# Norm's second half: where two weight remainders, two half-tile evictions and the up pairs' weight splits stand

## The chip, the cores and the metric

One core of a Trainium2 chip runs the whole program. The metric is the device time of one execution in microseconds (us); smaller is better. Five engines work in parallel, each through its own queue in program order: TensorE (PE: matrix multiplies, with its weight loads as PEld), VectorE (DVE), ScalarE (ACT), GpSimd (POOL) and SyncE (SP, which here only starts transfers). They meet at semaphores: an instruction waits until a counter has reached a value, and all that stands behind it on its queue waits too.

## The reference, cut

Two layers; each is a token mixer (projection `w_in`, three branches, gates, `w_out`), a layernorm, a gated feed-forward part with a causal convolution over three positions, and another layernorm. 512 prompt tokens and 64 sample tokens run through the same weights. What the change touches:

```python
def layernorm(x, g, b):
    mu = jnp.mean(xf, axis=-1, keepdims=True)
    xc = xf - mu
    var = jnp.mean(xc * xc, axis=-1, keepdims=True)
    return (xc * lax.rsqrt(var + LN_EPS) * g + b).astype(x.dtype)

def conv_ffn(h, prefix, w_up, conv_w, conv_b, w_down):
    a = h @ w_up                              # 1024 -> 2 * 2816
    ext = jnp.concatenate([prefix, a], axis=1)
    c = conv_b + conv_w[0] * ext[:, 0:T]
    for k in range(1, CONV_W):                # CONV_W = 3 taps
        c = c + conv_w[k] * ext[:, k:k + T]
    gate, up = jnp.split(c, 2, axis=-1)
    y = (jax.nn.silu(gate) * up) @ w_down
    return y, ext[:, -(CONV_W - 1):]

for l in range(2):
    x = layernorm(ALPHA * x + token_mixer(x), ln1_g[l], ln1_b[l])
    x = layernorm(ALPHA * x + conv_ffn(x), ln2_g[l], ln2_b[l])
```

## The kernel before, in words

**Layout.** Features lie on the 128 partitions, all 576 tokens on the free axis, in two token halves of 288. `X` is the residual stream in eight feature tiles (`X[:, k]`). Every large product is made three times in rounded fp32: a value is split into a rounded part (hi, made by ACT) and the remainder (lo, made by DVE), and PE adds w_hi x_hi, w_hi x_lo and w_lo x_hi. The split activations are `XH` and `XL` (both named m_XS in the trace).

**Weight units.** A 128-column slice of a weight matrix is one unit. SP fetches it into a raw buffer `WS`, ACT rounds it into `WH` (`weight_hi`, L548), DVE makes the remainder `WL` (`weight_lo`, L1434). A unit that uses raw buffer n is fetched once the remainder of the unit before it in that buffer is done. PE starts a tile when its remainder is there (`w_lo`), when the result bank of the tile's parity is free (`mm_free0` or `mm_free1`) and, in the first tile after a norm, row by row as `n_lo` counts up.

**Tiles.** A full tile is 8 rows x 2 token halves x 3 = 48 multiplies, a half tile 24.

**Norm, second half.** A norm runs token half by token half. While the second half is normalised, PE works on six half tiles of the next stage that only need the first token half: `first_halves`, with weight units u0 to u0+5. The next stage then begins with units u1 and u1+1. `first_halves` is called three times with a norm or an input: for the mixer input of layer 0 (no norm: the rows of x are only split), after norm 1 of each layer (next stage: the up projection), and after norm 2 of layer 0 (next stage: the input of layer 1). On DVE it runs `centre` (L1451, eight rows), `variance` (L1456), `inverse_root` (L1461), then `scaled` (L1468) and `normal_lo` (L1479) for each of eight rows, with the remainders of u0+4, u0+5, u1 and u1+1 strung between. On ACT it runs the squares (L574), the root (L579), `normal_hi` (L593; L548 where there is no norm) for the rows, and evicts each half tile: `stash` copies it to `STASH`, `first_half` copies it to `Z`.

**Up projection.** In up pair j, parity 0 is the gate tile and parity 1 the up tile. Pairs 0, 2 and 4 (`UP_FIRST`) had their first token half done in `first_halves`, so only a half tile of 24 multiplies is left of each; pairs 1, 3, 5 and all later ones are full. `up_tile` exists once on ACT (L940) and once on DVE (L1949). For each parity ACT copies the product to `EB` and rounds the weights of the next pair's tile of that parity; DVE then runs tap two (L1963), tap one (L1970) and tap zero (L1976) of the convolution into `CC`. ACT's Silu (L962) needs the gate half's last tap (`c_ready`). DVE multiplies (`HX`, L1984 and L1985), ACT rounds the product (`HH`), DVE takes its remainder (`HL`). The convolution of a parity starts when its `EB` copies are done, and those copies start when PE has ended the tile.

Of the kernel before, what the change touches and what calls it, by code (L numbers as in the profile page):

```python
# [13 lines left out]
D = 1024  # L14
# [92 lines left out]
def build(nc, x_t, x_save, cache_wide, page_table, branch_in, w_uk, w_ukt, w_uv, state_ffn_t, params,  # L107
# [3 lines left out]
    with ctx:  # L111
# [434 lines left out]
        def _(act):  # L546
# [72 lines left out]
            def first_halves(l, n, u0, m0, u1, evict):  # L619
# [24 lines left out]
                normal_hi(n, 1, (2, 3, 4))  # L644
                done(4)
                evict(4)
                normal_hi(n, 1, (5, 6, 7))
                done(5)
                evict(5)

            for l in range(DEPTH):
# [288 lines left out]
                def up_tile(hf, j, width, halved=None, last=False):  # L940
                    n0 = (l * 2 + hf) * FH + j
                    u0 = l * NU + U_FFN[hf] + 2
                    for par in range(2):
# [16 lines left out]
                        if par == 0:  # L960
                            act.wait_ge(S["c_ready"], n0 + 1)
                            nc.scalar.activation(SL[:, 0:CV - 2], CC[:, 0, 0:CV - 2], ACT.Silu)\  # L962
                                .then_inc(S["silu"], 1)
# [5 lines left out]
                for hf in range(2):  # L969
                    first = 2 * len(UP_FIRST) if hf == 0 else 0  # L970
                    for j in range(first):
                        up_tile(hf, j, D, UP_FIRST.index(j) if j in UP_FIRST else None)
# [459 lines left out]
        def _(dve):  # L1432
# [81 lines left out]
            def first_halves(l, n, u0, u1):  # L1514

                if n >= 0:
                    centre(n, 1, range(DT))
                    variance(n, 1)
                weight_lo(l * NU + u0 + 4)
                if n >= 0:  # L1520
                    inverse_root(n, 1)
                scaled(n, 1, 0)
                scaled(n, 1, 1)
                weight_lo(l * NU + u0 + 5)
                normal_lo(n, 1, 0)
                normal_lo(n, 1, 1)
                scaled(n, 1, 2)
                scaled(n, 1, 3)
                weight_lo(l * NU + u1)
                normal_lo(n, 1, 2)  # L1530
                scaled(n, 1, 4)
                normal_lo(n, 1, 3)
                scaled(n, 1, 5)
                normal_lo(n, 1, 4)
                scaled(n, 1, 6)
                normal_lo(n, 1, 5)
                scaled(n, 1, 7)
                normal_lo(n, 1, 6)
                normal_lo(n, 1, 7)
                weight_lo(l * NU + u1 + 1)  # L1540
# [27 lines left out]
            for l in range(DEPTH):  # L1568
# [380 lines left out]
                def up_tile(hf, j, width, halved=False, last=False):  # L1949
                    n0 = (l * 2 + hf) * FH + j  # L1950
                    u0 = l * NU + U_FFN[hf] + 2 * j
                    for par in range(2):
# [15 lines left out]
                        if halved:  # L1968
# [9 lines left out]
                        if par == 0:  # L1978
                            dve.drain().then_inc(S["c_ready"], 1)
                            if not halved:  # L1980
# [8 lines left out]
                    if not halved and not last:  # L1989
# [5 lines left out]
                for hf in range(2):  # L1995
# [4 lines left out]
                    for j in range(first):  # L2000
                        up_tile(hf, j, D, halved=j in UP_FIRST)
# [183 lines left out]
```

## Time and profile before

| | us |
|---|---|
| median of 3 runs | 2121.1 |
| lowest and highest run | 2120.16 and 2124.65 |
| span of the profiled execution | 2123.8 |
| TensorE busy in it | 2047.8 |
| VectorE busy | 1194.9 |
| ScalarE busy | 804.0 |
| GpSimd busy | 401.2 |

The profiled execution is one more execution of the same program, 2.7 us longer than the median. Busy time of a matmul is modelled and overlaps its neighbours, so a pause of PE between two tiles is a little longer, from start to start, than the idle time that a row gives. In the rows of the next but one section, the square bracket at the end of a row is the idle time of that engine just before the row and what ended it.

### The profile page before, as it was taken

To read this page: it belongs to the slowest core of one execution; us is meant where nothing else is said; L and a number is where in the kernel's file an instruction comes from. 1 tells how busy PE (TensorE), PEld (TensorE's weight loads), DVE (VectorE), ACT (ScalarE), POOL (GpSimd) and SP (SyncE) were. 2 spreads that over 40 slices of the span, in tenths; PEclk is the share of its full clock that TensorE was granted. 3 is DMA by queue.
4 is the path that set the end of the run, shared out by engine and by line. 5 is a ranking of instruction groups with operands and counts; after the bars stand their busy time and mean duration, and the time that the engine had idled before them with its cause. 6 is when DMAs were issued, how large, how long until landed. Compare 5 with 4: busy or idle time off the path is not lost.

```text
span 2123.8 us, 43041 instructions
## 1 busy us (share of the span) xinstructions
PE 2047.8 (96%) x17374; PEld 1891.6 (89%) x17374; DVE 1194.9 (56%) x2032; ACT 804.0 (38%) x1508; POOL 401.2 (19%) x407
## 2 busy tenths in 40 slices
PE   7999999999998999999999999999999999999997
PEld 7976667999998999999989766689999889999997
DVE  4764545333578652666758644453335876436665
ACT  4343434222354321334443443342223543223334
POOL 0026661000051000000350366600002600000012
PEclk9999999999999999999999999999999999999999
DMA  7349996222433232225452599942225232222252
GB/s 253 118 149 328 373 353 232 80 79 80 156 108 96 84 105 67 79 79 181 136 206 68 174 364 365 370 161 88 80 79 175 90 100 79 99 71 82 79 195 73
DMA packets 88850, 325.69 MB, mean 153 GB/s; under 512 B 10576, under 2 KB 15568, under 8 KB 88592
## 3 DMA queue, kind: packets, MB, share of 16 engines
q1 hardware_dynamic: 46512, 169.52, 24.4%
q0 software_dynamic: 37440, 144.98, 18.4%
q10 hardware_dynamic: 4768, 9.37, 1.4%
q8 instruction: 92, 1.51, 0.3%
q14 instruction: 38, 0.31, 0.0%
HBM read 315.52 MB, written 7.26 MB: 152 GB/s over the span
## 4 chain that ended last, share of the span: by engine, by line
PE 84%; DVE 8%; ACT 3%; DMA 2%; issue 1%; DVEq 1%; POOL 0%; PEldq 0%; SPq 0%; ACTq 0%; PEld 0%; POOLq 0%
PE PS L1010 65%; PE PS L1292 5%; PE PS L1262 5%; DVE m_WL L1434 3%; PE PS L1283 2%; DMA m_WS<-in_w_units 1%; PE PS L1273 1%; ACT m_WH L548 1%; DVE m_X L1468 1%; PE PS L1315 1%; DVE m_XS L1479 1%; PE PS L1041 1%; PE PS L1331 1%; PE PS L1322 1%; PE PS L1309 1%
## 5 line engine op out<-in xcount | busy, mean ns | idle before, releaser
L1010 PE MATMUL PS<-m_XS,m_WH 128*128 128x288 f32 x5120 | 922.0, 297 | 34.6 <-DVE m_WL L1434 18.0
L1010 PEld LDWEIGHTS PS<-m_XS,m_WH 128*128 128x128 f32 x5120 | 767.9, 189 | 43.7 <-DVE m_WL L1434 20.9
L1010 PE MATMUL PS<-m_XS,m_WL 128*128 128x288 f32 x2560 | 583.5, 297 | 0.0
L1434 DVE TENSOR_TENSOR m_WL<-m_WS,m_WH 128x1024 fp32r<-128x1024 f32 (+2 forms) x284 | 369.2, 1301 | 229.9 <-ACT m_WH L548 221.0
L548 ACT ACTIVATE m_WH<-m_WS 128x1024 fp32r<-128x1024 f32 (+2 forms) x284 | 315.6, 1113 | 374.6 <-PE PS L1010 341.1
L1010 PEld LDWEIGHTS PS<-m_XS,m_WL 128*128 128x128 f32 x2560 | 423.5, 189 | 0.0
L535 POOL DMA_INDIRECT m_RAW<-in_cache_wide,m_IDXS x256 | 242.4, 947 | 380.2 <-PE PS L1010 124.4
L478 POOL TENSOR_TENSOR m_XS<-m_X 128x288 f32<-128x288 f32 x8 | 10.6, 1320 | 1170.5 <-DVE m_X L1488 1169.5
L1010 PE MATMUL PS<-m_HH,m_WH 128*128 128x288 f32 x704 | 205.7, 299 | 5.2 <-DVE m_X L1488 4.9
L1010 PE MATMUL PS<-m_HL,m_WH 128*128 128x288 f32 x704 | 203.5, 296 | 0.0
L1010 PE MATMUL PS<-m_HH,m_WL 128*128 128x288 f32 x704 | 180.3, 297 | 0.0
L1010 PEld LDWEIGHTS PS<-m_HH,m_WH 128*128 128x128 f32 x704 | 133.0, 189 | 6.3 <-DVE m_WL L1434 5.3
L1010 PEld LDWEIGHTS PS<-m_HL,m_WH 128*128 128x128 f32 x704 | 133.2, 189 | 0.2
L1292 PE MATMUL PS<-m_RAW,m_PT 128*64 128x256 f32 x1024 | 124.6, 385 | 7.4 <-ACT m_PT L548 7.1
L1262 PE MATMUL PS<-m_RAW,m_QSF 64*64 64x256 f32 x1024 | 125.3, 382 | 0.9 <-DMA m_RAW<-in_cache_wide,m_IDXS 0.9
L1262 PE MATMUL PS<-m_RAW,m_QSR 64*64 64x256 f32 x1024 | 124.4, 382 | 0.0
L1010 PEld LDWEIGHTS PS<-m_HH,m_WL 128*128 128x128 f32 x704 | 123.2, 189 | 0.0
L1963 DVE TENSOR_SCALAR m_CC<-m_EB,m_PARS 128x592 f32<-128x592 f32 x88 | 51.9, 590 | 123.5 <-ACT m_EB L548 123.4
L1292 PEld LDWEIGHTS PS<-m_RAW,m_PT 128*64 128x64 f32 x1024 | 67.8, 136 | 47.8 <-ACT m_PT L548 14.6
L902 ACT ACTIVATE m_SIG<-PS 128x576 f32<-128x576 f32 x48 | 31.2, 650 | 185.7 <-PE PS L1010 185.7
L1786 DVE TENSOR_SCALAR_CACHE_REDUCE PS<-PS,m_NMX 128x512 f32<-128x512 f32 x64 | 48.5, 759 | 92.0 <-PE PS L1273 92.0
L1262 PEld LDWEIGHTS PS<-m_RAW,m_QSF 64*64 64x64 f32 x1024 | 69.0, 133 | 28.0 <-issue 16.1
(276 smaller groups left out, 2875.4 us busy)
## 6 DMA issues: line engine op xcount, KB each, us to landing
m_WS<-in_w_units SPq DMA_DIRECT2D x232, 512.0 KB
m_WS<-in_w_units SPq DMA_DIRECT2D x48, 704.0 KB
m_RAW<-in_cache_wide,m_IDXS POOLq DMA_INDIRECT x256
m_X<-in_x_t SPq DMA_DIRECT2D x6, 576.0 KB, 7.4
m_WS<-in_w_units SPq DMA_DIRECT2D x4, 576.0 KB
x_save<-m_X POOLq DMA_DIRECT2D x4, 576.0 KB, 4.4
m_X<-x_save SPq DMA_DIRECT2D x4, 576.0 KB, 6.9
out_y<-m_X SPq DMA_DIRECT2D x8, 288.0 KB, 2.2
```

The costliest lines, as they stand in the source:

```text
L535: pool.indirect_dma_start(raw_of(u)[:, q, :], None, cache_wide.rearrange("l n c -> (l n) c"), bass.IndirectOffsetOnAxis(ap=IDXS[:, l, g:g ...
L548: return nc.scalar.activation(out, in_, ACT.Copy)
L902: nc.scalar.activation(h2(SIG[:, g, :]), pair(g % 2), ACT.Sigmoid)\
L1010: mm = pe.matmul(out(half), w(part, k), x(k)[:, half_of(half)], start=(k == 0 and part == 0 and x is xh), stop=(k == last and part == 1))
L1041: mm = pe.matmul(PS[:, bank + h, 0:HT], C["ones"], x[:, h * HT:(h + 1) * HT], start=(k == 0), stop=(k == len(tiles) - 1))
L1262: pe.matmul(PS[64 * c:64 * c + 64, score_bank(u) + h, 0:256], weights, raw_of(u)[rows, c::2, at0:at0 + P], start=(g == 0), stop=False)
L1273: mm = pe.matmul(out[:, :, j, :], QSP[j][rows, rows_of], raw_of(u)[rows, c::2, 2 * KL:ROW], start=False, stop=(j == 1))
L1283: mm = pe.transpose(PS[:, 6, j * P:(j + 1) * P], PRB[:, j * P:(j + 1) * P], ident)
L1292: mm = pe.matmul(PS[64 * c:64 * c + 64, 7, 0:KL], PT[:, a, 64 * c:64 * c + 64], raw_of(u)[:, 2 * (a // 2) + c, j * KL:(j + 1) * KL], start ...
L1434: return dve.tensor_tensor(out, x, hi.bitcast(F32), ALU.subtract)
L1786: dve.tensor_scalar(s0, s0, -SCALE, NMX[:, b, j:j + 1], ALU.mult, ALU.min, accum_out=NMX[:, b, j + 1:j + 2]).then_inc(S["s_max"], 1)
L1963: dve.tensor_scalar(cc, e[:, 2:CV], tap(2), PARS[:, bass.ds(l * NPAR + C_CB + c, 1)], ALU.mult, ALU.add)
```

## The change

**Norm's second half, DVE.** The remainders of u0+4 and u0+5 move ahead of `variance`, that of u1 to right behind it. The rows follow in strict alternation, one `normal_lo` between two `scaled`, and the remainder of u1+1 moves from the end to ahead of the last two `normal_lo`.

**Norm's second half, ACT.** Half tile 4 is evicted after two rounded rows instead of five, half tile 5 after five instead of eight.

**Up pairs.** On DVE, pairs 0 to 5 of the first feed-forward half all take the weight remainders between tap two and tap one (before: pairs 0, 2 and 4 only). On ACT, Silu of these six pairs stands behind the up half's copies and weight rounding instead of behind the gate half's.

```diff
@@ first_halves, ACT
                 weight_hi(l * NU + u1 + 1)
                 normal_hi(n, 1, (0, 1))
-                normal_hi(n, 1, (2, 3, 4))
                 done(4)
                 evict(4)
-                normal_hi(n, 1, (5, 6, 7))
+                normal_hi(n, 1, (2, 3, 4))
                 done(5)
                 evict(5)
+                normal_hi(n, 1, (5, 6, 7))
@@ up_tile, ACT
-                        if par == 0:
+                        if par == (1 if silu_last else 0):
                             act.wait_ge(S["c_ready"], n0 + 1)
...
-                        up_tile(hf, j, D, UP_FIRST.index(j) if j in UP_FIRST else None)
+                        up_tile(hf, j, D, UP_FIRST.index(j) if j in UP_FIRST else None, silu_last=True)
@@ first_halves, DVE
                     centre(n, 1, range(DT))
+                weight_lo(l * NU + u0 + 4)
+                weight_lo(l * NU + u0 + 5)
+                if n >= 0:
                     variance(n, 1)
-                weight_lo(l * NU + u0 + 4)
+                weight_lo(l * NU + u1)
...
@@ up_tile, DVE
-                        up_tile(hf, j, D, halved=j in UP_FIRST)
+                        up_tile(hf, j, D, early=True)
```

On DVE after norm 1 of layer 0, behind the eight rows of `centre`, the queue is the following before; m_WL 152, 153, 154 and 155 are the remainders of u0+4, u0+5, u1 and u1+1.

```order
L1451 SCALAR_TENSOR_TENSOR m_X<-PS,m_X 128x288 x8
L1456 TENSOR_SCALAR m_RN<-PS 128x288
L1434 TENSOR_TENSOR m_WL_152<-m_WS_137,m_WH_144 128x1024
L1461 RECIPROCAL m_RN<-m_RN 128x288
L1468 SCALAR_TENSOR_TENSOR m_X<-m_X,m_PARS,m_RN 128x288 x2
L1434 TENSOR_TENSOR m_WL_153<-m_WS_138,m_WH_145 128x1024
L1479 SCALAR_TENSOR_TENSOR m_XS_50<-m_X,m_PARS,m_XS_50 128x288 x2
L1468 SCALAR_TENSOR_TENSOR m_X<-m_X,m_PARS,m_RN 128x288 x2
L1434 TENSOR_TENSOR m_WL_154<-m_WS_139,m_WH_146 128x1024
```

The same place after:

```order
L1451 SCALAR_TENSOR_TENSOR m_X<-PS,m_X 128x288 x8
L1434 TENSOR_TENSOR m_WL_152<-m_WS_137,m_WH_144 128x1024
L1434 TENSOR_TENSOR m_WL_153<-m_WS_138,m_WH_145 128x1024
L1456 TENSOR_SCALAR m_RN<-PS 128x288
L1434 TENSOR_TENSOR m_WL_154<-m_WS_139,m_WH_146 128x1024
L1461 RECIPROCAL m_RN<-m_RN 128x288
L1468 SCALAR_TENSOR_TENSOR m_X<-m_X,m_PARS,m_RN 128x288 x2
L1479 SCALAR_TENSOR_TENSOR m_XS_50<-m_X,m_PARS,m_XS_50 128x288
L1468 SCALAR_TENSOR_TENSOR m_X<-m_X,m_PARS,m_RN 128x288
```

Two remainders have passed the variance, a third the reciprocal, and none stands between the rows any more until the last two.

On ACT, behind the root of the same norm (m_WH_147 is u1+1 rounded), the queue is before:

```order
L548 ACTIVATE m_WH_147<-m_WS_140 128x1024
L593 ACTIVATE m_XS_50<-m_X,m_PARS 128x288 x5
L548 ACTIVATE m_STASH<-PS 128x288
L593 ACTIVATE m_XS_50<-m_X,m_PARS 128x288 x3
L548 ACTIVATE m_STASH<-PS 128x288
L938 ACT_TABLE_LOAD
```

and after:

```order
L548 ACTIVATE m_WH_147<-m_WS_140 128x1024
L593 ACTIVATE m_XS_50<-m_X,m_PARS 128x288 x2
L548 ACTIVATE m_STASH<-PS 128x288
L593 ACTIVATE m_XS_50<-m_X,m_PARS 128x288 x3
L548 ACTIVATE m_STASH<-PS 128x288
L593 ACTIVATE m_XS_50<-m_X,m_PARS 128x288 x3
L938 ACT_TABLE_LOAD
```

Each of the two evictions has moved ahead of three rounded rows.

On DVE in up pair 1 of layer 0, which is a full pair, the queue is before (m_WL_152 and m_WL_153 are the remainders for pair 2, parities 0 and 1):

```order
L1963 TENSOR_SCALAR m_CC<-m_EB,m_PARS 128x592
L1965 COPY m_TAIL<-m_EB 128x2
L1970 SCALAR_TENSOR_TENSOR m_CC<-m_EB,m_PARS,m_CC 128x592
L1972 COPY m_TAIL<-m_EB 128x16
L1976 SCALAR_TENSOR_TENSOR m_CC<-m_EB,m_PARS,m_CC 128x592
L1434 TENSOR_TENSOR m_WL_152<-m_WS_137,m_WH_144 128x1024
L1963 TENSOR_SCALAR m_CC<-m_EB,m_PARS 128x592
```

and after:

```order
L1964 TENSOR_SCALAR m_CC<-m_EB,m_PARS 128x592
L1966 COPY m_TAIL<-m_EB 128x2
L1434 TENSOR_TENSOR m_WL_152<-m_WS_137,m_WH_144 128x1024
L1971 SCALAR_TENSOR_TENSOR m_CC<-m_EB,m_PARS,m_CC 128x592
L1973 COPY m_TAIL<-m_EB 128x16
L1977 SCALAR_TENSOR_TENSOR m_CC<-m_EB,m_PARS,m_CC 128x592
L1964 TENSOR_SCALAR m_CC<-m_EB,m_PARS 128x592
```

The remainder has moved ahead of tap one; in parity 1 of the pair it moves likewise, from behind `HX` to ahead of tap one.

## Rows read from the trace of the kernel before

**Rows 1.** The page: busy time, share of the span and instructions of each engine.

```profile
PE 2047.8 (96%) x17374; PEld 1891.6 (89%) x17374; DVE 1194.9 (56%) x2032; ACT 804.0 (38%) x1508; POOL 401.2 (19%) x407
```

**Rows 2.** Timeline, PE, layer 0's up stage: start, us, engine, line, operation, [idle before].

```profile
639.76 0.51 PE L1010 MATMUL PS<-m_XS,m_WH 128*128 128x288 f32 x2 [1.67 <-issue]
...
644.42 0.54 PE L1010 MATMUL PS<-m_XS,m_WH 128*128 128x288 f32 x2 [0.47 <-DVE m_WL L1434]
...
661.25 0.54 PE L1010 MATMUL PS<-m_XS,m_WH 128*128 128x288 f32 x2 [0.72 <-DVE m_WL L1434]
...
666.16 0.54 PE L1010 MATMUL PS<-m_XS,m_WH 128*128 128x288 f32 x2 [1.45 <-DVE m_WL L1434]
...
687.91 0.54 PE L1010 MATMUL PS<-m_XS,m_WH 128*128 128x288 f32 x2 [2.06 <-DVE m_WL L1434]
```

**Rows 3.** Timeline, DVE, norm's second half, layer 0.

```profile
628.65 0.46 DVE L1456 TENSOR_SCALAR m_RN<-PS 128x288 f32<-128x288 f32 x1 [6.10 <-PE PS L1063]
...
643.15 1.22 DVE L1434 TENSOR_TENSOR m_WL<-m_WS,m_WH 128x1024 fp32r<-128x1024 f32 x1
```

**Rows 4.** Timeline, ACT, same place.

```profile
625.46 1.06 ACT L548 ACTIVATE m_WH<-m_WS 128x1024 fp32r<-128x1024 f32 x1
...
639.27 0.39 ACT L548 ACTIVATE m_STASH<-PS 128x288 f32<-128x288 f32 x1
```

**Rows 5.** Chain that ended last, in order of time, at layer 1's input.

```profile
1071.23 4.95 DMA m_WS<-in_w_units
...
1082.94 5.89 PE PS L1010 x24
```

**Rows 6.** Timeline, layer 1's input: DVE's variance, ACT's rounding of u1+1, PE.

```profile
1069.53 0.46 DVE L1456 TENSOR_SCALAR m_RN<-PS 128x288 f32<-128x288 f32 x1 [6.37 <-PE PS L1063]
...
1076.20 1.06 ACT L548 ACTIVATE m_WH<-m_WS 128x1024 fp32r<-128x1024 f32 x1 [3.11 <-DMA m_WS<-in_w_units]
...
1082.94 0.82 PE L1010 MATMUL PS<-m_XS,m_WH 128*128 128x288 f32 x2 [3.59 <-issue]
```

**Rows 7.** Windows: us, busy (and count) of PE, PEld, DVE, ACT, POOL; clock, DMA, GB/s.

```profile
689.10:692.40 3.30, 3.30 (x16) 3.30 (x15) 2.89 (x4) 0.22 (x2) 0.00 (x0) 0.50 0.69 197
...
1081.60:1088.40 6.80, 5.46 (x23) 5.49 (x24) 6.41 (x10) 2.73 (x6) 6.46 (x7) 0.50 0.55 178
...
1736.00:1741.00 5.00, 2.93 (x22) 2.76 (x21) 4.79 (x9) 2.43 (x6) 0.00 (x0) 1.00 0.31 96
```

**Rows 8.** Windows of PE alone: us, busy (count), clock; a half tile at either clock.

```profile
661.20:664.50 3.30, 3.25 (x24) 1.00 0.48 159
...
687.90:692.70 4.80, 4.79 (x24) 0.64 0.55 160
```

**Rows 9.** Timeline, DVE, up pair 1 of layer 0, parity 1, then pair 2.

```profile
661.49 0.59 DVE L1963 TENSOR_SCALAR m_CC<-m_EB,m_PARS 128x592 f32<-128x592 f32 x1 [0.29 <-ACT m_EB L548]
...
662.23 0.84 DVE L1970 SCALAR_TENSOR_TENSOR m_CC<-m_EB,m_PARS,m_CC 128x592 f32<-128x592 f32 x1
...
664.15 0.69 DVE L1984 TENSOR_TENSOR m_HX<-m_SL,m_CC 128x512 f32<-128x512 f32 x1
...
664.89 1.22 DVE L1434 TENSOR_TENSOR m_WL<-m_WS,m_WH 128x1024 fp32r<-128x1024 f32 x1
...
667.47 1.23 DVE L1434 TENSOR_TENSOR m_WL<-m_WS,m_WH 128x1024 fp32r<-128x1024 f32 x1
```

**Rows 10.** Timeline, ACT, same place: HH, then copies and rounding for pair 2.

```profile
665.01 0.68 ACT L548 ACTIVATE m_HH<-m_HX 128x576 fp32r<-128x576 f32 x1 [2.68 <-DVE m_HX L1985]
665.60 0.20 ACT L548 ACTIVATE m_EB<-m_SFT 128x16 f32<-128x16 f32 x1
...
666.38 1.06 ACT L548 ACTIVATE m_WH<-m_WS 128x1024 fp32r<-128x1024 f32 x1
```

**Rows 11.** Timeline, layer 0's input: ACT's eviction of half tile 5, DVE's last rows.

```profile
34.85 0.41 ACT L548 ACTIVATE m_Z<-PS 128x288 f32<-128x288 f32 x1 [0.90 <-PE PS L1010]
...
33.00 2.29 DVE L1434 TENSOR_TENSOR m_XS<-m_X,m_XS 128x288 fp32r<-128x288 f32 x6
```

More of the change, by code:

```diff
@@ L938, in _, with up_tile @@
                 nc.scalar.preload_act_table(ACT.Silu)
-                def up_tile(hf, j, width, halved=None, last=False):
+                def up_tile(hf, j, width, halved=None, last=False, silu_last=False):
                     n0 = (l * 2 + hf) * FH + j
@@ L1523, in first_halves @@
                 scaled(n, 1, 1)
-                weight_lo(l * NU + u0 + 5)
                 normal_lo(n, 1, 0)
+                scaled(n, 1, 2)
                 normal_lo(n, 1, 1)
-                scaled(n, 1, 2)
                 scaled(n, 1, 3)
-                weight_lo(l * NU + u1)
                 normal_lo(n, 1, 2)
@@ L1537, in first_halves @@
                 scaled(n, 1, 7)
+                weight_lo(l * NU + u1 + 1)
                 normal_lo(n, 1, 6)
                 normal_lo(n, 1, 7)
-                weight_lo(l * NU + u1 + 1)
             def split_in(half, k):
@@ L1948, in _, with up_tile @@
                     dve.memset(EB[:, par, 0:2], 0.0)
-                def up_tile(hf, j, width, halved=False, last=False):
+                def up_tile(hf, j, width, early=False, last=False):
                     n0 = (l * 2 + hf) * FH + j
@@ L1967, in up_tile @@
                         dve.drain()
-                        if halved:
+                        if early:
                             weight_lo_in_loop(u0 + 2 + par, par, width)
@@ L1979, in up_tile @@
                             dve.drain().then_inc(S["c_ready"], 1)
-                            if not halved:
+                            if not early:
                                 weight_lo_in_loop(u0 + 2, 0, width)
@@ L1988, in up_tile @@
                         .then_inc(S["h_ready"], 1)
-                    if not halved and not last:
+                    if not early and not last:
                         weight_lo_in_loop(u0 + 3, 1, width)
```

## The prediction

> **What bounds the kernel now.** First the page: TensorE is busy 96% of the span, DVE 56%, ACT 38% [rows 1]. The products are untouched, so only PE's pauses and its clock can change. The PE timeline names the pauses in reach: in layer 0's up stage 1.67, 0.47, 0.72, 1.45 and 2.06 us, smaller ones aside [rows 2]; layer 1 repeats them. The third place is layer 1's input: the chain there runs through a weight fetch of 4.95 us, and then one half tile on PE takes 5.89 us instead of 3.3 [rows 5, 8]. Its PE row has 3.59 us idle before it [rows 6]. So some 18 us in all, 0.8% of the time, can be won.
>
> The windows show the clock beside it. Two stretches ran at 0.50, that is 1.2 of 2.4 GHz: 689.1 to 692.4, behind the pause of 2.06, and 1081.6 to 1088.4, from inside the pause of 3.59. Layer 1's twin of the first pause kept 1.00, with 2.93 of 5 us busy [rows 7]. A half tile takes 4.8 us where such a stretch falls on it, 3.3 where not [rows 8]: 1.5 us each.
>
> **Part 1: norm's second half, after norm 1 (two layers).** DVE idles 6.10 us between the eight centred rows and the variance [rows 3]. The rounding of u0+5 ends at 626.5 [rows 4], so two remainders of 1.22 are done by 627.8, before the variance at 628.65: cost nothing, the wait for PE hides them. The third takes the place of the first behind the variance. The rows start as before, at 632.2. Then one remainder instead of three stands between them and their end at 643.2 [rows 3]; of the two, the one that stood last was behind the rows and doesn't shorten them, the other gives 1.14, and about 0.4 of that is lost because the first rounded row still stands behind ACT's rounding of u1+1. Rows end at 642.5.
>
> ACT: half tile 4 is evicted at 639.27 in before although PE had ended it by 635 [rows 4]; PE waited for the bank until 639.76, though it was free at 637.9 (639.76 less 1.67, less 0.17 that a follower starts before the modelled end). Now the eviction follows two rounded rows, at 635.0. PE runs six of eight rows of up tile (0,0) at once and waits 1.7 us for row 6. It ends at 642.9; the remainder of u1+1 is ready by 641.4. Tile (0,1) starts at 642.9 instead of 644.42 [rows 2]: **-1.5**. The next tile's remainder comes 3.5 us after the end of (0,0), 0.1 to 0.2 late: **-1.4 per layer** is left. Eviction 5 (0.39) delays rounded row 5 to 639.0, which DVE reads at 639.1: hidden, with 0.1 to spare.
>
> **Part 2: up pairs 0 to 5.** In pair 1 the early remainders of the gate half start pair 2's first tile without the 0.72, and ACT, no longer held by Silu, has the up half's ready too, without the 1.45. From start to start these pauses are 0.9 and 1.6: -2.5. But DVE's work is only reordered, and what stands behind it is pair 2's own eviction. Before, DVE goes from tap two at 661.49 over tap one (662.23) and the product (664.15) to ACT's HH (665.01); then follow the copies for pair 2 (665.60), the rounding (666.38) and the remainder (667.47 to 668.70) [rows 9, 10]. The end of tile (1,1) was at 660.4: 8.3 us. Now the remainder that stood at 664.89, beside ACT's HH, stands ahead of tap one and inside that chain: +1.17, so 9.5. In these 9.5 us PE has only the two half tiles of pair 2, 6.6 us [rows 8]. So pair 3 waits **3.0 us** (2.7 to 3.3), where before it waited for nothing: two small pauses become one long one, +0.5. Pair 4 and 5 repeat it, +0.5. Pair 6, which by these steps waited 0.3 before, saves that. Sum per layer +0.7, with part 1 -0.7. Silu moved on ACT costs nothing: the up half's remainder and taps on DVE, 3 us, hide its 0.7; without them it would add 0.6 a pair.
>
> In layer 0 the stretch of half clock at 689.1 was paid before (1.5, of which it hid a 0.3 pause): if nothing took its place, layer 0 would have -1.9, layer 1 -0.7.
>
> **Part 3: layer 1's input.** The fetch at 1071.23 starts when the remainder of u0+4 is done [rows 5]. That remainder, at 1069.9 before, moves to the start of DVE's pause of 6.37, to 1063.2. The weights land at about 1069.4; ACT, which waited 3.11 for them, reaches their rounding at 1073.1 instead of 1076.20 [rows 6]. The rows then end at 1083.5 instead of 1086.8, PE starts at 1079.2 with the bank free, and with it the pause and the half clock go: the half tile ends at 1084.0 instead of 1088.8. A bound from the same rows: DVE's steps there were up to 0.5 longer twice, which costs 1.0 more, and a stretch of half clock would take 1.5. **-4.5** (-3.0 to -5.0). What follows is chained to this tile through ACT's rounding and SP's fetches, so it is kept.
>
> **Part 4: layer 0's input.** No norm is waited for here, and the eviction of half tile 5 is at 34.85, when PE ends it [rows 11]. Three rounded rows now stand behind it (0.41 + 3 x 0.35), so the last is ready at 36.4; with the remainder of 1.22 and two rows behind it DVE ends at 38.1, before at 35.3. PE wants the last row at 37.4: **+0.7**, and the later remainder fetches the next unit later: I take +0.8 (0 to +1.3).
>
> **Sum without clock:** +0.8 - 4.5 - 1.9 - 0.7 = -6.3.
>
> **The clock on the new pauses.** Four pauses of 3.0 us are new. The rows beside: the pause of 3.59 was followed by half clock, of the two of about 2.06 one was and one wasn't [rows 2, 6, 7]. So three of four seems likeliest, at 1.5: **+4.5**. The bounds are 0 (none) and, by the stretch of 6.8 us behind the 3.59, two stretches behind each.
>
> The Trainium skill, page "TensorE: Matmul & The Clock Gate", section "Why this matters for your kernels", asks for no idle gaps of more than about 3 us between bursts. The trace disagrees in part, since 2.06 us idle was enough once. By the page alone, before's pauses in the up stage would cost nothing and the new ones would stand right at its limit; taken as just over it four times, the sum would be about 0. By the page taken as just under, it is the first rival.
>
> **Sum:** -6.3 + 4.5 = -1.8. The profiled execution (2123.8) would become 2122.0; it had the same share of half clock as I count, and its 2.7 us over the median I carry for both kernels alike. The median 2121.1 becomes **2119.3**.
>
> **Rivals.**
> - *The long pauses stay at full clock* (none or one drops). For: layer 1's pause of 2.07 did. Against: 3.0 is nearer to 3.59. -6.3 to -4.8, so 2114.8 at best. 0.19.
> - *The early split removes the pauses and makes none*, because HH or the copies of pair 2 don't wait as counted. Then both layers lose another 6.1 (2 x 3.05) and all half clock: -18.5, 2102.6. Against: HH's row idles 2.68 for HX, so the chain is real [rows 10]. 0.06.
> - *Slower: two stretches of half clock behind each new pause.* Place: pair 3's and pair 5's tiles. Price: up to 3.4 us each, half of 6.8 [rows 7], 13.6 in all: +7.3, 2128.4. It decides from 2.6 us a pause ((6.3 + 4.2) / 4). Against: at 1082.94 the half tile lost only 2.4 us, as part of the stretch lay in the pause. 0.06.
> - *The change doesn't do what it says:* the remainders moved ahead of the variance hold it up, since ACT's rounding of u0+5 is late. It ends at 626.5, 0.9 us more than a remainder before the variance [rows 3, 4], and the same in layer 1; DVE would have to lose that 0.9 first, and a loss of 1 us a norm (+3) would stay within the forecast's case.
>
> **How the numbers follow.** The forecast, two to four half-clock stretches, has 0.69 and spans -3.3 to -0.3 by itself; with the bounds of parts 3 and 4 it is 2116.5 to 2122.5. The range reaches to the first rival and leaves out the two others and the tails: 2114.0 to 2123.0. A measurement tells 0.2%, 4.2 us, from no change. Faster by more than that is the first rival nearly whole and the second: 0.25. Slower 0.06. Same 0.69.
>
> **What would show it.** Layer 1's input: no 3.59 pause, ACT's rounding of u1+1 near 1073, the half tile ended 4 to 5 us earlier. PE's row at 639.76 with no pause before it, one of 1.5 to 1.8 inside that tile. In pair 2 no pauses, before pair 3's and pair 5's first tiles about 2.8 us idle in a row, ended by m_WL. Windows behind these four: 0.5 in three. It is wrong if pair 3 starts without a pause, if layer 1's input wins under 3 us, or if half clock shows in none.

## The result and the profile after

| | before | after |
|---|---|---|
| median, us | 2123.18 | 2126.06 |
| lowest and highest | 2117.99, 2126.32 | 2120.8, 2131.14 |
| runs | 20 | 20 |
| span of the profiled execution | 2123.8 | 2122.2 |

The ratio after to before is 1.0016 [1.0008, 1.0023]: 3.4 us slower. That is less than 0.2%, so it lies in the case called "same", but the interval leaves 1 out and the sign is not the one forecast (-1.8). The range (2114.0 to 2123.0) does not hold 2126.06. Of the 6.8 us between 2119.3 and 2126.06, 2.1 come from the base: with 20 runs the kernel before has a median that much above that of the three runs from which the forecast started. The other 4.7, the difference of the two medians (2.9) less the forecast -1.8, are the forecast's own.

The two profiled executions alone would say the reverse: after has the shorter span. Single executions of either kernel lie up to 5 us from its median, and the sections below say in part why. Below, means with their standard errors are therefore given beside medians: after's 20 runs have a mean of 2126.0 ± 0.65. Three slow executions among the experiments below, two of before (7036.39 and 3339.99 us) and one of e7 (4100.34), stand in no mean and no ratio.

The page of after, busy time of each engine and the group of the tiles' first multiplies (busy, mean ns | idle before them, and what ended most of it):

```profile
PE 2045.4 (96%) x17374; PEld 1890.3 (89%) x17374; DVE 1196.0 (56%) x2032; ACT 804.9 (38%) x1508; POOL 405.6 (19%) x407
...
L1010 PE MATMUL PS<-m_XS,m_WH 128*128 128x288 f32 x5120 | 921.9, 297 | 36.1 <-DVE m_WL L1434 21.8
```

Same counts, nearly the same busy times as [rows 1]. Timeline of PE in after, the pauses in the order in which the steps named them (start, us, ..., [idle just before, what ended it]):

```profile
38.23 0.54 PE L1010 MATMUL PS<-m_XS,m_WH 128*128 128x288 f32 x2 [0.67 <-DVE m_XS L1434]
...
641.00 0.54 PE L1010 MATMUL PS<-m_XS,m_WH 128*128 128x288 f32 x2 [1.50 <-DVE m_XS L1479]
...
667.81 1.33 PE L1010 MATMUL PS<-m_XS,m_WH 128*128 128x288 f32 x4 [2.91 <-DVE m_WL L1434]
...
691.51 1.33 PE L1010 MATMUL PS<-m_XS,m_WH 128*128 128x288 f32 x4 [2.92 <-DVE m_WL L1434]
...
1084.76 0.54 PE L1010 MATMUL PS<-m_XS,m_WH 128*128 128x288 f32 x2 [1.74 <-DVE m_XS L1479]
...
1715.48 1.33 PE L1010 MATMUL PS<-m_XS,m_WH 128*128 128x288 f32 x4 [2.91 <-DVE m_WL L1434]
...
1739.28 1.33 PE L1010 MATMUL PS<-m_XS,m_WH 128*128 128x288 f32 x4 [2.91 <-DVE m_WL L1434]
```

The pauses of 0.72, 1.45 and 2.06 of [rows 2] are gone. In their place stand four of 2.9 idle, 3.07 from start to start, before the first tile of pairs 3 and 5 in both layers. The pause of 1.67 has moved into the first tile, before its row 6. The 3.59 of [rows 6] is 1.74. At 38.23 is a pause that before did not have.

Windows of after behind these four pauses (us, busy (count) of PE, PEld, DVE, ACT, POOL; granted clock, DMA share, GB/s):

```profile
667.80:675.50 7.70, 7.69 (x48) 7.69 (x49) 6.43 (x12) 1.82 (x3) 0.00 (x0) 0.81 0.45 138
...
667.30:670.70 3.40, 2.89 (x12) 2.89 (x13) 3.04 (x7) 1.64 (x2) 0.00 (x0) 0.50 0.46 143
...
691.20:694.60 3.40, 3.09 (x13) 3.09 (x14) 3.05 (x7) 1.44 (x2) 0.00 (x0) 0.50 0.48 149
1715.20:1718.60 3.40, 3.12 (x13) 3.12 (x14) 3.03 (x7) 1.41 (x2) 0.00 (x0) 0.50 0.52 152
1739.10:1742.50 3.40, 3.22 (x13) 3.22 (x14) 3.03 (x7) 1.31 (x2) 0.00 (x0) 0.50 0.49 154
```

Each of the four is followed by 3.4 us at 0.50, that is 1.2 of 2.4 GHz. Pair 3's first tile, 48 multiplies, takes 7.6 us by it instead of 6.3.

Stages of the two traces, from multiply to multiply:

| stage | before | after | difference |
|---|---|---|---|
| layer 0's input, first tile | 3.20 | 4.12 | +0.9 |
| layer 0, first up tiles, end of (1,0) | 16.12 | 15.02 | -1.1 |
| layer 0, from there to (6,0) | 57.65 | 60.13 | +2.5 |
| layer 1's input, the whole projection | 48.85 | 45.12 | -3.7 |
| layer 1, first up tiles | 16.10 | 15.53 | -0.6 |
| layer 1, up pairs | 56.62 | 60.28 | +3.7 |

Together about +1.7 in these two executions, where the spans differ by -1.6. The rest is in part half clock behind pauses that both kernels have and that one execution caught and the other did not: before has stretches at 566 and 1617.5, after has them at 22 and 995. Another 1.2 of it after wins between 300 and 566 us, in a stage that the change doesn't touch.

### The profile page after: what moved, and what is told of

Its sections match the earlier page's. It is cut to its first block, busy times and chain, and to the rows that moved or that the text cites. A ratio compares the mean times of both kernels' runs of the same rounds, so it can differ in the third digit from the quotient of the medians.

```text
span 2122.2 us, 43041 instructions
## 1 busy us (share of the span) xinstructions
PE 2045.4 (96%) x17374; PEld 1890.3 (89%) x17374; DVE 1196.0 (56%) x2032; ACT 804.9 (38%) x1508; POOL 405.6 (19%) x407
## 4 chain that ended last, share of the span: by engine, by line
PE 84%; DVE 8%; ACT 4%; DMA 2%; issue 1%; DVEq 1%; PEldq 0%; ACTq 0%; POOL 0%; SPq 0%; PEld 0%; POOLq 0%
PE PS L1010 64%; PE PS L1292 5%; PE PS L1262 5%; DVE m_WL L1434 3%; ACT m_WH L548 2%; PE PS L1283 2%; PE PS L1273 1%; DMA m_WS<-in_w_units 1%; PE PS L1315 1%; PE PS L1331 1%; DVE m_XS L1479 1%; DVE m_X L1468 1%; PE PS L1041 1%; PE PS L1322 1%; PE PS L1309 1%
```

## The experiments

**Theory A.** The norm part wins, the up pairs' part loses more, and it loses through the clock: the pause of 3.07 is followed by half clock nearly always. **Theory B.** The clock behind the new pauses is chance as behind the old ones and costs nothing net; the loss is in the norm part or in the pauses' own length. (The expectations call Theory A "C" and Theory B "N"; their "I" is the rival that the two parts hinder one another, and the "A" of e13 says that the parts add.) The comparisons below are each with before's runs on the same chip in the same session: 5 to 12 of the kernel, 15 to 35 of before.

| kernel | median, us | ratio to before | mean less before's mean |
|---|---|---|---|
| norm part alone (e1) | 2118.47 | 0.9984 [0.9971, 0.9997] | -4.0 |
| up part alone (e2) | 2125.61 | 1.0015 [1.0005, 1.0025] | +3.2 |
| after, pauses filled (e3) | 2118.83 | 0.998 [0.9968, 0.9992] | -4.1 |
| second remainder late (e4) | 2119.69 | 0.9988 [0.9975, 1.0001] | -2.6 |
| after again (e5) | 2123.82 | 1.0005 [0.9992, 1.0017] | +1.7 |
| all together (e6) | 2109.92 | 0.9946 [0.9928, 0.9965] | -11.3 |
| before, pauses filled (e7) | 2119.14 | 0.9982 [0.997, 0.9994] | -3.3 |
| e6, up pairs filled only (e8) | 2112.33 | 0.9962 [0.9948, 0.9976] | -8.4 |
| after, filled by four (e11) | 2125.48 | 1.0009 [0.9998, 1.0019] | +1.1 |
| e6 with more filled (e12) | 2113.82 | 0.995 [0.9936, 0.9964] | -10.0 |
| after, third session (e13) | 2125.9 | 1.0009 [0.9998, 1.0019] | +2.0 |
| norm part, again (e14) | 2119.79 | 0.9986 [0.9976, 0.9995] | -3.4 |
| up part, again (e15) | 2128.6 | 1.0026 [1.0017, 1.0034] | +5.3 |
| least edit (e16) | 2113.19 | 0.9949 [0.9935, 0.9962] | -10.7 |

The standard error of a kernel's mean here is 0.5 to 1.3 us, of the difference about 1. Against what was expected, e1 won 1 to 2 us less and e2 lost 2 to 4 less, e7 won less (3.3, not 4 to 6), e6 and e8 won more (11.3 for 7 to 10, 8.4 for 5 to 7), and e12 won nothing beyond e6.

### The two halves apart

**e1_norm_only**: against after, the norm's new order on DVE and ACT, the up pairs as before.

```diff
-                        if par == (1 if silu_last else 0):
+                        if par == 0:
...
-                        up_tile(hf, j, D, early=True)
+                        up_tile(hf, j, D, halved=j in UP_FIRST)
```

> Part of the change alone: norm's second half in the new order on DVE and ACT, the up pairs as before. Theory C (the clock makes the difference to the forecast: all of the four new pauses are followed by half clock): without those pauses this part keeps what its steps say, +0.9 at layer 0's input, -4.2 at layer 1's, -1.4 in each up stage, so -5 to -6 us against the kernel before. Theory N (the norm part brings less than its steps say, for instance because layer 0's input or the chained fetches take it back): -2 us or less. Trace: up tile (0,1) starts 1.5 us sooner after the end of half tile 5, and pair 2's pauses of 0.7 and 1.5 are still there.

**e2_up_only**: the reverse, against after: `first_halves` as before, the up pairs as after.

```diff
+                normal_hi(n, 1, (2, 3, 4))
                 done(4)
                 evict(4)
-                normal_hi(n, 1, (2, 3, 4))
+                normal_hi(n, 1, (5, 6, 7))
                 done(5)
                 evict(5)
-                normal_hi(n, 1, (5, 6, 7))
...
+                    variance(n, 1)
                 weight_lo(l * NU + u0 + 4)
-                weight_lo(l * NU + u0 + 5)
-                if n >= 0:
-                    variance(n, 1)
-                weight_lo(l * NU + u1)
...
```

> The other part alone: up pairs 0 to 5 with the early remainders and the late Silu, norm's second half as before. Theory C: +0.8 of pauses per layer and four stretches of half clock at 1.4 us where before had one on average, so +5 to +7 us against the kernel before. Theory N: pauses +0.7 a layer and about the same clock as before, +1 to +2 us. Trace: about 2.9 us idle ahead of pair 3's and pair 5's first tile in both layers, no pause in pair 2 and 4.

Measured: -4.0 and +3.2. The timeline of PE in e1 at the two places, the first in up pair 4, the second at layer 1's input:

```profile
686.35 0.53 PE L1010 MATMUL PS<-m_XS,m_WH 128*128 128x288 f32 x2 [2.07 <-DVE m_WL L1434]
```

```profile
1081.56 0.54 PE L1010 MATMUL PS<-m_XS,m_WH 128*128 128x288 f32 x2 [1.75 <-DVE m_XS L1479]
```

Norm's part alone takes the pause of 3.59 away as after does, and keeps the old pauses of the up pairs. In e2 the 3.6 at layer 1's input is still there with 6.8 us of half clock, and the four of 3.07 have come. So the gain is all in one half and the loss all in the other: Theory B's first form falls.

### The new pauses, filled

**e3_after_filler**: after, with twelve multiplies whose result nobody reads, in the result bank 5, ahead of the two tiles that wait.

```diff
+            def filler(n):
+                for i in range(n):
+                    pe.matmul(PS[:, 5, 0:HT], XH[:, i % DT, 0:P], XH[:, i % DT, 0:HT], start=True, stop=True)
...
+                            if (j, par) in ((3, 0), (5, 0)):
+                                filler(12)
```

> The changed kernel with 12 multiplies whose result nobody reads on PE, just ahead of pair 3's and pair 5's first tile in each layer, 1.6 us of each pause of 3.0; nothing else moves and the tile starts as late as before. Theory C: the idle rest of 1.4 us is followed by no half clock, so 4 x 1.4 and some double stretches go: 6 to 8 us less than the changed kernel, -3 to -5 us against the kernel before. Theory N: the clock had little part, within 1.5 us of the changed kernel. Trace: window behind the pause at 1.00, the full tile of 48 in 6.3 us instead of 7.6.

**e11_filler_4**: the same with `filler(4)`.

```diff
-                                filler(12)
+                                filler(4)
```

> The changed kernel with 4 idle multiplies ahead of pair 3's and pair 5's first tile instead of 12: of the pauses of 3.0 us 2.5 stay. The cost of the clock by length of pause: with 12 (1.5 us idle left) it was gone, 6.6 us for the four pauses. If the cost grows with the length from about 2, this one lies between, 2 to 3 us less than the changed kernel, at that of the kernel before (within 2 us). If a pause of 2.5 costs what 3.0 costs, +2.5 as the changed kernel.

Timeline of PE in e3, the idle multiplies and the tile behind them, then the windows of pause and tile:

```profile
663.78 1.74 PE L1098 MATMUL PS<-m_XS 128*128 128x288 f32 x12
666.86 0.80 PE L1010 MATMUL PS<-m_XS,m_WH 128*128 128x288 f32 x4 [1.34 <-DVE m_WL L1440]
```

```profile
663.50:666.80 3.30, 2.02 (x16) 1.79 (x14) 2.65 (x5) 3.30 (x11) 0.00 (x0) 1.00 0.03 12
666.80:673.00 6.20, 6.14 (x46) 6.14 (x47) 5.68 (x11) 1.19 (x2) 0.00 (x0) 1.00 0.40 114
```

The tile waits for the same remainder until the same moment; only the idle time has shrunk from 2.91 to 1.34, and the clock stays at 1.00 and the tile takes 6.3 us. e3 comes out at -4.1, the same as the norm part alone in its session (-4.0). That settles the mechanism: with pauses as long as before but filled, the up part costs nothing, so its loss is clock. How much is less sure. After itself, over its three sessions (44 runs), is at +2.4, which makes the idle multiplies worth 6.5 us; in e3's own session, where after did not run, the up part lost 3.2, which makes them worth 3.3. So a pause costs 0.8 to 1.6 us through the clock. With four multiplies 2.39 idle are left, and the trace shows half clock behind two of four:

```profile
691.22 0.80 PE L1010 MATMUL PS<-m_XS,m_WH 128*128 128x288 f32 x4 [2.39 <-DVE m_WL L1440]
```

Its +1.1 ± 1.3 lies between after (+2.4) and e3 (-4.1) and can be told neither from after nor from the half-way point.

### The cover of one remainder

**e4_late_second**: in pairs 1, 3 and 5 the up half's remainder goes back behind `HX`, beside ACT's `HH`, where before had it.

```diff
-                        if early:
+                        if early and (par == 0 or j in UP_FIRST):
...
-                    if not early and not last:
+                    if not (early and j in UP_FIRST) and not last:
```

> The changed kernel, but in pairs 1, 3 and 5 the second remainder stands behind HX again (beside ACT's HH), the first one stays ahead of tap one and Silu stays late. The chain that makes the pause of 3.0 us: 1.17 shorter, so pair 3 and 5 start without a pause, and the pause stands ahead of pair 2's and pair 4's second tile instead, at 2.5 from start to start. Both theories: 0.55 less pause per pair, 2.2 us less than the changed kernel in pauses. Theory C adds: pauses of 2.5 are followed by half clock about half as often as those of 3.0, another -2 to -3; in all 4 to 5 us less than the changed kernel. Theory N: 2 us less.

DVE and PE at this place in e4, timelines:

```profile
660.98 0.22 DVE L1986 TENSOR_TENSOR m_HX<-m_SL,m_CC 128x64 f32<-128x64 f32 x1
661.12 1.22 DVE L1434 TENSOR_TENSOR m_WL<-m_WS,m_WH 128x1024 fp32r<-128x1024 f32 x1
662.25 0.75 DVE L1434 TENSOR_TENSOR m_HL<-m_HX,m_HH 128x576 fp32r<-128x576 f32 x1
```

```profile
662.39 0.85 PE L1010 MATMUL PS<-m_XS,m_WH 128*128 128x288 f32 x2 [2.44 <-DVE m_WL L1434]
```

The remainder lies again in the time in which ACT rounds `HH`, and no tile of pair 3 or 5 waits. One pause of 2.6 a pair of pairs is left instead of 3.07. The trace had half clock behind all four of them, where half as often as behind 3.0 was expected, so the order alone does not free the clock. It gains 4 to 6 us against after (-2.6 where after has +1.7 to +3.2), less than 1 of them clock by the mean granted clock of the runs. The shorter pauses explain 2 of them; for the others no cause is shown. Against the norm part alone in its session (-4.0) it loses 1.4 ± 1.4, with pauses of nearly the same sum but merged.

### After again, and whether the halves add up

**e5_after_again** and **e13_both_parts**: the changed kernel itself, in two further sessions, with no edit.

> The changed kernel once more, on the chip of the kernels beside it. The two parts alone gave -4.0 and +3.2 us in the mean against the kernel before, which adds to -0.8, while the whole gave +3.2. Theory C (clock): parts add, and the whole against before is between -1 and +3, with some 14 to 15 us of time lost to the half clock by the granted clock of each run. Theory I (the two parts hinder one another): +3 again or more, with pauses in the trace that neither part alone has.

> The changed kernel, beside its two parts on one chip. Theory A (parts add, sessions scatter): the whole is within 1.5 us of the sum of the two parts beside it, and the three granted clocks fit. Theory I (the whole loses more by the clock than the parts): 3 us or more above the sum, with at least 2 us more lost by granted clock than the parts' losses add to.

**e14_norm_part** and **e15_up_part**: the edits of e1 and of e2 once more, in the session of e13.

> The norm part alone once more, for the sum. By its stages: +0.9, -3.7 and twice -0.8, less one of the two stretches of half clock at layer 1's input: -4 against the kernel before.

> The up pairs' part alone once more, for the sum. By its stages: +0.8 of pauses a layer and 1.6 for each of the four new pauses, less what the pauses of before lost to the clock (about 2.5): +5 against the kernel before; +3.2 was measured.

In the first two sessions the halves (-4.0 and +3.2) summed to -0.8, the whole +3.2 (the 20 runs above) and +1.7; an interaction was possible. In one session they give -3.4 and +5.3, sum +1.9, and the whole +2.0. The halves add, within an error of 1.3. Between the sessions the up part differs by 2.1, with an error of about 1.2, and e5 shows what can carry that: behind the same pause the clock can be low for twice as long.

```profile
664.00:667.10 3.10, 0.20 (x2) 0.00 (x0) 2.67 (x5) 3.10 (x11) 0.00 (x0) 0.87 0.01 3
666.30:673.10 6.80, 5.97 (x25) 5.97 (x26) 6.28 (x11) 1.96 (x4) 0.00 (x0) 0.50 0.35 95
```

In the five traces of kernels with these pauses (after, e2, e5, e13, e15) there are 20 of them: 14 were followed by 3.4 us at 0.50, three by 6.8, three by none.

### Which edit of the norm part wins

**e9_evict_only**: before with ACT's hunk alone.

```diff
-                normal_hi(n, 1, (2, 3, 4))
                 done(4)
                 evict(4)
-                normal_hi(n, 1, (5, 6, 7))
+                normal_hi(n, 1, (2, 3, 4))
                 done(5)
                 evict(5)
+                normal_hi(n, 1, (5, 6, 7))
```

> Of norm's second half only ACT's edit, the two evictions between rounded rows; DVE's queue as before. If the bank was what PE waited for, up tile (0,0) starts 1.8 us sooner and (0,1) about 1.5 sooner. By the steps of the queues the rows come next: DVE ends its last row at the same time as before, so tile (0,0) starts sooner, waits inside, and (0,1) starts within 0.2 us of before. At layer 1's input the rows bind too (the weights still land at 1076), 1 us won at most because the multiplies are spread and the half clock falls on fewer.

**e10_dve_only**: before with DVE's hunk of `first_halves` alone.

```diff
+                weight_lo(l * NU + u0 + 4)
+                weight_lo(l * NU + u0 + 5)
+                if n >= 0:
                     variance(n, 1)
+                weight_lo(l * NU + u1)
...
```

> Of norm's second half only DVE's edit; ACT's queue as before. If the evictions mattered, the gain in the up stage is gone. By the steps of the queues nothing is lost: ACT reaches the eviction of half tile 4 at 637.4 on the clock of before since its rows come sooner, so (0,1) starts 1.3 to 1.5 us sooner and layer 1's first half tile ends about 4 us sooner, as with both edits; and layer 0's input keeps the time of before, 0.9 less than with both, since no rounded row waits behind half tile 5.

Both were executed once, so the places are compared and not the totals (2131.18 and 2118.17). PE in the first up tile of layer 0, timelines of e9, then of e10:

```profile
640.97 0.53 PE L1010 MATMUL PS<-m_XS,m_WH 128*128 128x288 f32 x2 [0.21 <-DVE m_XS L1479]
642.08 0.54 PE L1010 MATMUL PS<-m_XS,m_WH 128*128 128x288 f32 x2 [0.45 <-DVE m_XS L1479]
643.18 0.54 PE L1010 MATMUL PS<-m_XS,m_WH 128*128 128x288 f32 x2 [0.44 <-DVE m_XS L1479]
```

```profile
640.89 0.54 PE L1010 MATMUL PS<-m_XS,m_WH 128*128 128x288 f32 x2 [1.40 <-DVE m_XS L1479]
```

With the bank free sooner but DVE's rows as late as before, PE only waits in small pieces for `normal_lo`: the tile ends no sooner. With DVE's order alone it ends as in after (the first two up tiles: 9.80 before, 8.31 after, 8.09 in e10), and the start of layer 1's input wins the same (8.42 in after, 8.40 in e10, 13.01 before, 11.92 in e9). At layer 0's input e9 and e10 both keep the 3.20 of before; only both edits together make the 4.12. So beside DVE's order the evictions' move adds nothing and costs the 0.9; alone it wins nothing in the up stage and 1.1 at layer 1's input.

In e9 half clock came behind the waits of 0.44 to 0.47 in this tile and right behind it; there was no longer one. Window:

```profile
646.00:649.40 3.40, 3.40 (x15) 3.40 (x16) 2.72 (x5) 1.29 (x3) 1.91 (x2) 0.51 0.47 154
```

Layer 1's twin of these waits was followed by none. So no single long pause is needed for it.

### The pauses that both kernels have

**e7_before_filler**: before, with seven idle multiplies ahead of the up halves of pairs 2 and 4, and eight ahead of the last row of `w_out` and `w_down`.

```diff
+                            if (j, par) in ((2, 1), (4, 1)):
+                                filler_up(7)
...
+                filler(8, SPLIT_OF[u0])
```

> The kernel before with only such idle multiplies added: 7 ahead of pair 2's and pair 4's second tile, 8 in the pauses of the output projections. All its waits stay. Theory C: of its 12 us lost to half clock about 5 stay (layer 1's input, start, end), 4 to 6 us less than the kernel before. Without a clock effect: the same as before within 1 us.

**e6_all**: the norm's new order where there is a norm, the old one at layer 0's input; the first remainder early in all six pairs, the second only in pairs 0, 2, 4 (as e4); ten idle multiplies at the same place in pairs 2 and 4, eight in `w_out` and `w_down`.

```diff
-                normal_hi(n, 1, (5, 6, 7))
+                normal_hi(n, 1, (5, 6, 7) if n < 0 else (2, 3, 4))
...
+                        if early and (par == 0 or j in UP_FIRST):
...
+                                filler_up(10)
...
+                filler(8, SPLIT_OF[u0])
```

> A version put together from what the runs showed: norm's second half in the new order where there is a norm, in the old order at layer 0's input (-0.9 there); first remainder early in all six pairs, second early only in pairs 0, 2 and 4; Silu late; and PE multiplies whose result nobody reads in the pauses: 10 ahead of pair 2's and pair 4's second tile, 8 ahead of the last row of both kinds of output projection (pauses of 2.2 and 2.6). Theory C: only the stretches at layer 1's input (sometimes) and at the start and end are left, so 7 to 10 us less than the kernel before. Theory I or no clock effect: -2 to -3.

**e8_up_filler**: e6 without the eight in `w_out` and `w_down`.

```diff
-                filler(8, SPLIT_OF[u0])
```

> As the version put together, but without the idle multiplies in the output projections; only the 10 ahead of pair 2's and pair 4's second tile. Theory C: 5 to 7 us less than the kernel before, 2 to 3 more than the version with both. It tells how much of the gain the up stage alone holds.

**e12_all_more**: e6 with twelve there, and eight ahead of row 6 of the first tile behind each norm.

```diff
-                filler(8, SPLIT_OF[u0])
+                filler(12, SPLIT_OF[u0])
...
+                    if fill and k == DT - 2:
+                        filler_up(8)
```

> The version put together, with idle multiplies also inside the first tile after each norm, ahead of its row 6 (8 of them, pauses of 1.7 and 1.9), and 12 instead of 8 in the output projections, whose rest of 2.0 was still followed by half clock in one of two cases. If the clock is all that is left there, 1 to 3 us less than the version put together, 13 to 14 less than the kernel before; if not, the same as that.

**e16_small**: before with DVE's norm order alone, seven idle multiplies in pairs 2 and 4, twelve in `w_out` and `w_down`; ACT and the up pairs' order untouched.

```diff
+                weight_lo(l * NU + u0 + 4)
+                weight_lo(l * NU + u0 + 5)
...
+                                filler_up(7)
...
+                filler(12, SPLIT_OF[u0])
```

> VectorE's order of the norm alone (ScalarE and the up pairs as in the kernel before), with 7 idle multiplies ahead of pair 2's and pair 4's second tile and 12 in the output projections. If the clock and the norm order are the whole gain: within 2 us of the version put together, 9 to 11 us less than the kernel before. If Silu's and the remainders' place mattered: 3 us or more behind it.

Before with its pauses filled wins 3.3 us with no other edit: before too pays for its clock. e6 wins 11.3, e8 8.4; the fillers of the output projections are worth about 2.9 ± 1.2. e12 has 8 idle multiplies more behind each norm and 4 more in each output projection, and is not faster than e6 (-10.0 to -11.3, in two sessions, each ± 0.6 to 0.9), although its runs had 2.5 us of low clock against 5.6 (one less granted clock, times the time, pauses included). The idle multiplies are not what cost it: the first two up tiles take 8.32 us in both traces. One difference is to be seen: e6's trace has two stretches in which PE goes through its tiles 2% faster at the same granted clock, e12's has none. Windows of equal length in the up pairs' loop of layer 1, e6, then e12:

```profile
1830.00:1850.00 20.00, 20.00 (x155) 20.00 (x154) 5.49 (x5) 3.49 (x3) 0.00 (x0) 1.00 0.22 73
1830.00:1850.00 20.00, 20.00 (x150) 20.00 (x150) 4.76 (x4) 2.76 (x2) 0.00 (x0) 1.00 0.28 90
```

Windows of e12 over the places of the up pairs and the projection, and the one stretch of half clock left, in which PE has nothing to do:

```profile
661.00:664.00 3.00, 1.86 (x14) 1.63 (x13) 2.89 (x7) 2.42 (x6) 0.00 (x0) 1.00 0.14 16
683.00:688.00 5.00, 3.88 (x29) 3.65 (x28) 4.81 (x10) 2.56 (x8) 0.00 (x0) 1.00 0.35 108
987.00:991.00 4.00, 2.70 (x21) 2.50 (x21) 4.00 (x6) 2.65 (x2) 0.00 (x0) 1.00 0.63 196
2107.80:2112.00 4.20, 0.00 (x0) 0.00 (x0) 1.22 (x3) 1.79 (x5) 0.00 (x0) 0.50 0.80 281
```

e16 gets within 1 us of e6 (0.6 ± 1.3, in another session) with a fraction of the edits. Its PE rows in pairs 2 and 4, where before had 1.45 and 2.06 idle:

```profile
663.51 0.53 PE L1010 MATMUL PS<-m_XS,m_WH 128*128 128x288 f32 x2 [0.52 <-DVE m_WL L1445]
...
685.26 0.54 PE L1010 MATMUL PS<-m_XS,m_WH 128*128 128x288 f32 x2 [1.13 <-DVE m_WL L1445]
```

Both e6 and e16 are faster than before by 0.5%, and than after by somewhat more.

## Why the prediction was wrong in sign

Sorted by halves, the forecast was -6.5 for the norm and the inputs (parts 1, 3 and 4: -2.8, -4.5, +0.8) and +4.7 for the up pairs (twice +0.7, less 1.2 for the old stretch, +4.5 for the clock). The halves alone measure -3.7 (e1 and e14) and +4.2 (e2 and e15), each ± 0.7. So the step that failed is the size of the norm's half, 2.8 us: above all part 3, the -4.5 that was to be kept at layer 1's input, and then part 1, the -1.4 per layer. The up half is not refuted as a sum, but the runs leave it open between 4.2 and 6.1 (after's +2.4 less the norm's -3.7).

The stages of the traces say where. Thirteen have DVE's new norm order, four have the old order on both engines (before, e2, e15, e7); e9 belongs to neither:

| stage, mean over traces, us | old | new | difference | forecast |
|---|---|---|---|---|
| layer 1's input, the whole projection | 48.58 | 45.71 | -2.9 | -4.5 |
| first up tiles, layer 0 | 16.11 | 15.19 | -0.9 | -1.4 |
| first up tiles, layer 1 | 16.13 | 15.23 | -0.9 | -1.4 |
| layer 0's input, both edits | 3.20 | 4.13 | +0.9 | +0.8 |

That sums to -3.8, beside the -3.7 of the runs.

- **Part 1, the norm.** PE's first two up tiles end 1.5 us sooner as stated (9.80 to 8.31), and the pause of 1.67 is inside the first, at 641.00, with 1.50 idle. At the end of (1,0) 0.5 to 1.2 of it is left instead of 1.4. The evictions, named as half of the cause, are not needed (e9, e10).
- **Part 3, layer 1's input.** The mechanism is right: the pause of 3.59 and its half clock are gone, ACT rounds u1+1 at 1074.85 in after, whose variance is 1.6 later than before's, so at 1073.2 on before's clock where 1073.1 was forecast. The first tile wins 4.2 (9.47 to 5.26), but over the projection 3.7 are kept and not 4.5. That the gain is kept since what follows is chained is the step that failed. The half clock itself was no accident of one trace: all four traces with the old order have 6.8 us of it there. But the chain runs on through a weight fetch. A fetch of this chain took 6.89 us in after; one took 8.30 in e5 and one 8.02 in e14, and then PE waited anew, before another tile, with half clock behind the wait. Those two keep 0.8 and 1.1 us of the gain (48.01 and 47.74 against 48.85). The chain in e5, then PE's row:

```profile
1088.47 8.30 DMA m_WS<-in_w_units
...
1099.23 0.53 PE L1010 MATMUL PS<-m_XS,m_WH 128*128 128x288 f32 x2 [2.19 <-DVE m_WL L1434]
```

The forecast put no such wait and no half clock behind the new tile; 3 of the 13 traces have half clock in this projection (e5, e14, e8). A gain under 3 us here was one of the prediction's own signs of being wrong: after has 3.7, the traces' mean is 2.9.
- **Part 4, layer 0's input.** +0.9 where +0.8 was taken. Right, and the same in all eight traces of kernels with both norm edits there.
- **Part 2, the up pairs.** The chain through `HX`, `HH` and the copies is as counted: pauses of 3.07 where 3.0 was forecast, four of them, ended by m_WL. The rest of the up stage lost 0.9 to 1.2 a layer where 0.7 was counted: 2.5 less 1.3 of clock (two stretches of 1.4, one of 1.5 gone) in layer 0, 3.7 less 2.8 in layer 1.
- **The clock.** "Three of four, at 1.5", 4.5 in all. The traces show 17 of 20, three of these for 6.8 us, and e3 measures 3.3 to 6.5 for the four. The count was near; the long stretch was put into a rival of 0.06 as if it fell on all or none, where it belongs to the average. Against this the old pauses of 2.1 to 2.2 were followed by half clock in 5 of 8 cases (before, e1, e10, e14), so their removal gives back about 1.9 and not 1.2. In the traces' mean the up pairs lose 3.6 us in layer 0 and 2.3 in layer 1 (five traces with the new pauses, four with the old), 5.9 where 4.7 was forecast.
- **The rivals.** The long pauses at full clock would have been -6.3; e3, which has that clock, is at -4.1, so the steps outside the clock were 2 us too generous as well. The slower rival, two stretches behind each pause, has the right mechanism and too large a price. "The change doesn't do what it says" falls by every row above: the variance row in after waits 0.79 for PE's sums, not for a remainder.

```profile
1071.15 0.46 DVE L1456 TENSOR_SCALAR m_RN<-PS 128x288 f32<-128x288 f32 x1 [0.79 <-PE PS L1063]
```

The remaining miss is of another kind. One trace was read as the kernel's time. Of its stretches of half clock the forecast priced those that this execution happened to have, and it carried the profiled run's 2.7 us over a three-run median that was itself 2.1 low. With the measured halves (-3.7 + 4.2) on the 20-run median, the sum is 2123.7, where 2126.06 was measured in that session and +1.7 and +2.0 over before in the two others. Over all 44 runs after is 2.4 slower; the halves by the stages of the traces (-3.8 and +5.9) give +2.1, so 2.7 of the forecast's own 4.7 are the norm's half and 1.2 the up half. The halves' own runs sum to 1.9 less than the whole; this has an error of about 1.2, and no cause of it is shown.

What stays open: whether a pause of 2.4 (e11) costs clearly less than one of 2.9, what decides between none, 3.4 and 6.8 us of half clock behind the same pause, and what Silu's new place does by itself, since no run moves it alone.

The Trainium skill, page "TensorE: Matmul & The Clock Gate", section "Why this matters for your kernels", warns of idle gaps above about 3 us. The pauses of after have 2.91 idle and were followed by half clock in 17 of 20 cases, those with 2.06 idle in 5 of 8; the measurement decides.

## What to carry to other kernels

A reordering that merges short pauses of TensorE has to be priced with the clock: here 0.9 and 1.6, and 0.3 and 2.2, became 3.07 each, and besides the 0.6 more in length each cost 0.8 to 1.6 us through the clock. Whether merging at the same sum costs anything is not shown (e4: 1.4 ± 1.4). Where a pause cannot be removed, fill it with multiplies whose result nobody reads, until about 1.3 us are left: no half clock followed the eight such rests in e3, e12 and e16. It took nothing from the kernel's work and won 3 us on the unchanged kernel, 3 to 6.5 on the changed one, and with DVE's new norm order 11 in all. A gain at the head of a chain that runs on through weight fetches is not kept for certain: look for the next wait. Where the clock drops in some executions and not in others, price every pause by its frequency over several traces, and take the base from some 20 runs, since three of them were 2 us off.

## What the hardware showed that was not expected

- The clock does not fall every time. The same instruction stream, the same pause to 0.02 us, was followed by nothing, by 3.4 us or by 6.8 us at 0.50 in different executions.
- The clock alone does not make the spread of one kernel's runs (2120.8 to 2131.1): e3's runs, the four new pauses filled, spread by 10.3 too, and e16's six by 5.8. In 8 of the 18 traces PE also goes through a long run of full tiles 2% faster at a granted clock of 1.00: 171 multiplies from 1850.96 us in e13 take 22.52 us, where the same ones take 22.99 in after. That wins some 3 us in a layer. It is not the instruction stream: e13 has it and after, the same kernel, has not. What brings it is not shown. Windows of equal length, after, then e13:

```profile
1830.00:1850.00 20.00, 20.00 (x151) 20.00 (x151) 4.76 (x4) 2.76 (x2) 0.00 (x0) 1.00 0.30 96
1830.00:1850.00 20.00, 20.00 (x154) 20.00 (x153) 4.76 (x4) 2.76 (x2) 0.00 (x0) 1.00 0.28 93
```

- The stretch can begin inside the pause (at 667.3 for a tile that starts at 667.81, at 666.3 in e5), so a part of it costs nothing.
- Idle multiplies are cheap: 12 of 128x288 took 1.74 us in the pause and moved the waiting tile by nothing, since it waits for DVE: from start to start the pause is 3.07 to 3.09 in e3, 3.07 in after.
